# The last expert stage reads its stationary tiles as even and odd tokens instead of first and last 128

## What is computed

```python
ue = u_tab[eid]
a = jax.nn.gelu(jnp.einsum('thkd,td->thk', ue, xb).astype(jnp.float32))
ve = v_tab[eid]
return jnp.einsum('thk,thkd->td', (g * a).astype(xb.dtype), ve)
```

## Time and profile before

| | us |
|---|---|
| median of 3 runs | 2239.63 (2239.49 to 2239.93) |
| the profiled execution | 2239.02 |
| its span in the profile | 2237.3 |
| TensorE busy (PE) | 2216.5, 99% of the span |
| weight loads busy (PEld) | 2082.9, 93% |
| VectorE, ScalarE, GpSimd busy | 1704.3, 1353.4, 854.4 |

### The profile page before, as it was taken

One profiled execution on the slowest core, in us unless ns is written; L12 is line 12 of the kernel. 1 busy time (PEld: TensorE's weight loads), 2 busy tenths in 40 slices (PEclk: granted clock), 3 DMA queues, 4 the chain that ended last, 5 costly groups with the idle time before them and its releaser, 6 DMA issues.

```text
span 2237.3 us, 49289 instructions
## 1 busy us (share of the span) xinstructions
PE 2216.5 (99%) x15792; PEld 2082.9 (93%) x15792; DVE 1704.3 (76%) x3283; ACT 1353.4 (60%) x2705; POOL 854.4 (38%) x766
## 2 busy tenths in 40 slices
PE   8999999999999999999999999999999999999998
PEld 8999999999999888888999999999999998888887
DVE  6556768976888788788874567699578888888887
ACT  6544546667777555555764545566677775555555
POOL 3100108988777122121032001099877771221210
PEclk9999999999999999999999999999999999999999
DMA  6444554555444789888555445455554448898884
GB/s 225 162 143 164 168 181 160 188 186 181 159 159 160 259 306 324 271 304 298 176 187 164 141 166 188 137 189 187 183 178 159 159 161 284 311 321 267 306 279 138
DMA packets 127141, 462.94 MB, mean 207 GB/s; under 512 B 14704, under 2 KB 14864, under 8 KB 126288
## 3 DMA queue, kind: packets, MB, share of 16 engines
q1 hardware_dynamic: 106416, 385.20, 49.1%
q0 software_dynamic: 20640, 76.68, 12.1%
HBM read 457.87 MB, written 3.95 MB: 206 GB/s over the span
## 4 chain that ended last, share of the span: by engine, by line
PE 96%; DVE 2%; ACT 1%; issue 1%; POOLq 0%; POOL 0%; ACTq 0%; DVEq 0%
PE ps L1436 21%; PE ps L1441 20%; PE ps L1437 20%; PE ps L1674 10%; PE ps L1675 10%; PE ps L1676 10%; PE ps L1630 1%; PE ps L1631 1%; PE ps L1589 1%; PE ps L1552 0%; DVE w_lo L875 0%; POOLq L324 0%; DVE h_lo L914 0%; PE ps L1554 0%; PE ps L1535 0%
## 5 line engine op out<-in xcount | busy, mean ns | idle before, releaser
L398 POOL TENSOR_TENSOR w_lo<-raw,w_hi 128x512 fp32r<-128x512 f32 x508 | 644.9, 1292 | 251.9 <-ACT w_hi L499 156.3
L1436 PE MATMUL ps<-h_hi,w_hi 128*128 128x256 f32 (+1 forms) x2592 | 651.2, 289 | 10.1 <-DVE h_lo L856 7.9
L1437 PE MATMUL ps<-h_lo,w_hi 128*128 128x256 f32 (+1 forms) x2592 | 638.3, 282 | 0.0
L1436 PEld LDWEIGHTS ps<-h_hi,w_hi 128*128 128x128 f32 x2592 | 489.3, 189 | 11.5 <-issue 9.3
L1437 PEld LDWEIGHTS ps<-h_lo,w_hi 128*128 128x128 f32 x2592 | 487.8, 188 | 0.2
L477 ACT ACTIVATE w_hi<-raw 128x1024 fp32r<-128x1024 f32 x334 | 351.8, 1053 | 190.5 <-PE ps L1441 189.7
L1244 DVE TENSOR_TENSOR w_lo<-raw,w_hi 128x512 fp32r<-128x512 f32 x504 | 347.6, 690 | 120.4 <-ACT w_hi L725 83.0
L875 DVE TENSOR_TENSOR w_lo<-raw,w_hi 128x1024 fp32r<-128x1024 f32 x208 | 256.5, 1233 | 186.7 <-ACT w_hi L477 185.7
L1674 PE MATMUL ps<-w_hi,h_hi 128*128 128x512 f32 x1016 | 395.2, 389 | 0.0
L1676 PE MATMUL ps<-w_hi,h_lo 128*128 128x512 f32 x1016 | 395.2, 389 | 0.0
L1675 PE MATMUL ps<-w_lo,h_hi 128*128 128x512 f32 x1016 | 395.2, 389 | 0.0
(11 more groups left out here) (225 smaller groups left out, 2973.5 us busy)
## 6 DMA issues: line engine op xcount, KB each, us to landing
raw<-stream SPq DMA_DIRECT2D x730, 512.0 KB, 3.4
bias<-bias_in POOLq DMA_DIRECT2D x2, 1152.0 KB, 6.9
x_keep<-x POOLq DMA_DIRECT2D x2, 1152.0 KB, 5.3
x<-x_keep POOLq DMA_DIRECT2D x2, 1152.0 KB, 10.5
x<-x_in SPq DMA_DIRECT2D x4, 288.0 KB, 4.6
y_out<-t_op SPq DMA_DIRECT2D x4, 288.0 KB, 2.1
ws<-ws_in POOLq DMA_DIRECT2D x2, 512.0 KB, 4.2
ring<-u_rows,rows POOLq DMA_INDIRECT x44, 6.5
```

Of the source, the lines that this page charges most:

```text
L398: return pool.tensor_tensor(w_lo[:, k % 2, lo_col:hi_col], raw[:, k, lo_col:hi_col], w_hi[:, k % 2, lo_col:hi_col].bitcast(F32), ALU.subtract)
L1436: pe.matmul(out, wh, rhs_hi, start=first, stop=False)
L1437: pe.matmul(out, wh, rhs_lo, start=False, stop=False)
```

## The change

Tile 0 becomes the tokens 0, 2, 4, ..., 254 and tile 1 the tokens 1, 3, ..., 255. The stationary operand of every matmul of the stage is then 128 columns at a step of two (8 bytes apart), spread over the 1024 bytes of all 256 tokens. The moving operand, the PSUM banks, the number, shape and order of the instructions and all waits stay. `v_sum` holds even tokens in tile 0 and odd ones in tile 1; `turn` writes each transpose to every second column of its 256 PSUM columns, which puts the tokens back in order. What reads these columns is unchanged.

```diff
+                def every_second(tokens, tile):
+                    return tokens.rearrange("p (n i) -> p i n", i=TILES)[:, tile, :]
+
                 def expert_unit(q, j, e, first=False, last=False):
...
                         for tile in range(TILES):
-                            at = slice(tile * P, tile * P + P)
-                            m_up = m_first[:, 0, at] if first else mixed_hi[L][j][:, at]
-                            m_low = m_first[:, 1, at] if first else mixed_lo[L][j][:, at]
+                            m_up = every_second(m_first[:, 0, :] if first else mixed_hi[L][j], tile)
+                            m_low = every_second(m_first[:, 1, :] if first else mixed_lo[L][j], tile)
...
                 def turn(c):
                     out = ps[:, OUT_BANK[c], :]
                     for tile in range(TILES):
-                        pe.transpose(out[:, tile * P:tile * P + P], v_sum[:, tile, c * P:c * P + P], ident[:, :])
+                        pe.transpose(every_second(out[:, 0:SEQ], tile), v_sum[:, tile, c * P:c * P + P], ident[:, :])
```

## The result

| | median, us | runs |
|---|---|---|
| kernel before | 2239.78 (2239.49 to 2240.06) | 4 |
| changed kernel | 2260.12 (2259.99 to 2260.51) | 4 |

The ratio is 1.009, with a 95% interval of 1.0078 to 1.0102. The change costs 20.3 us. The time lies inside the range that was given, on the other side from the forecast.

A forecast was written before the change was run, and what follows sets the result against it. TensorE's distance between matmul starts was taken to bound the kernel. 2239.0 - 34 (loads) + 0 (transposes) = 2205.0 us, given as 2206 since the median of the runs stands 0.6 us higher; range 2199 to 2276.

The forecast's parts named there:

- What bounds the kernel: TensorE, busy 99% of the span; the last expert stage, 696.4 us, bound only by 226.7 ns between matmul starts.
- What the 226.7 ns are made of: Last expert stage: 213.3 ns for 512 columns plus 13.4 ns, of which about 11 ns disturbance between load and stream.
- the plain f32 rows: Plain f32 matmuls of 288 columns: 242.3 ns, only 2.3 ns over their columns; read as load and stream at one pace.
- The hint from the earlier trace: First unit of the stage, tiles from `m_first` 32 bytes off: 233 ns instead of 226.7, taken as a hint, no proof.
- The load: Stationary loads at step two, 3072 times: distance falls from 226.7 to 215.6 ns, 34 us gained.
- two readers at one pace: Load at step two walks 8 bytes in two cycles like the stream; they meet once, then no more: 11.1 ns less.
- the price doubles: Rival, slower (0.32): load and stream conflict per line or stretch, the wider walk has twice as many; 237.8 ns, 2274 us.
- half price: Half of the extra cost in the rival of conflicts per line or stretch: kernel time 2257 us.
- a load that takes twice as long: Last expert stage: at most 233.4 ns per matmul, 6.7 ns over the distance before, 21 us lost.
- Nothing changes: Rival, unchanged (0.20): the 11 ns are a fixed cost of changing a float32r tile, wherever it lies; 2239 to 2243 us.
- The transposes: 32 transposes writing every second PSUM column: taken as 0, at most 3.5 us lost.
- what is late next: VectorE, ScalarE and the DMA queue keep up with a stage of 331 us instead of 348, so the gain stays.

The follow-up runs named there:

- map_pair: Last expert stage with still tiles; upper and lower parts, second tile and moving operand moved separately: 213.4 to 220.0 ns per matmul at 480 columns, 226.7 to 233.3 at 512.
- the scan: Last expert stage with tiles from a still part of SBUF, starts moved within 256 bytes: step one 226.7 to 234.3 ns per matmul, step two 229.9 to 233.5.
- map_plain: Same tiles and streams read as plain f32, several steps and places: 429.2 ns at 512 columns; at 256 columns 215.8 ns, at step 4 233.3.
- before_moved_32: Kernel before, with only the four buffers of mixed_hi and mixed_lo moved by 32 bytes: 2260.18 us, ratio 1.0089.
- map_place: Last expert stage with still tiles at chosen steps and starts: step one 226.7 or 233.3 ns unmoved or moved 32 bytes, step two unmoved 233.3, step 8 244.4.

## Why the prediction was wrong, step by step

**What bounds the kernel** was right: the distance between two starts in that stage, and nothing else, carried the whole change, 3072 x 6.6 = 20.3 us.

**What the 226.7 ns are made of** was right in part. 213.3 ns belong to the columns, and what comes on top depends on how the two readers lie to each other (map_pair). But at steps one and two the runs move it only between 13.3 and some 22 ns. That 11 of the 13.3 ns of the kernel before are disturbance too was taken over from the plain f32 rows; at 512 columns no float32r variant fell below 226.7 ns, so this is not shown. The hint from the earlier trace rows was a good one: `m_first` lies 32 bytes off, and that place cost 233.3 ns in the scan too.

**The load is the step that failed.** The prediction held that two readers at one pace meet once and do not meet again, and took the plain f32 matmuls of the earlier trace rows for the proof. Those are undisturbed whatever the pace: with a stream that takes a column every second cycle, steps one, two and four all stand at 429.2 ns (map_plain). The equal pace was one of several differences between the rows that were compared, and the runs show that it was not the one that mattered. With a step of two the float32r distance was 229.9 to 233.5 ns at all 35 places tried, 14 to 18 ns over the 215.6 that were forecast. The load's pace itself, two cycles per column, was an upper bound (116.7 ns over 128 columns) taken for a value; no run measures it.

**The rival 'the price doubles'** had the sign and half of the size (6.6 of 11.1 ns; its half price, 2257, was 3 us off). Its mechanism, price per stretch, falls: the same price appears without any step after a move of 32 bytes. What the prediction did not list is what happened: the kernel before lay at one of the few cheap places, and the new arrangement left it. The row that could have said so was there: one unit at another place, 233 ns, and 6.3 ns dearer. It was used against another reading, and not asked what it would make of the sum by itself: 3072 x 6.3 = 19 us, close to the measured 20.3.

**Luck.** The prediction also priced a load that takes twice as long: at most 233.4 ns and 21 us lost. These are nearly the measured figures, but not for that reason: the load is recorded at 194 ns against 188, and before_moved_32 lost the same 20 us with loads at step one.

**'Nothing changes'** rested on the load costing nothing more, and on the 13.3 ns being fixed; they went to 20.0. The two rules of the Trainium skill behind it fare differently. The Trainium skill, SBUF — State Buffer, Specifications (TRN2), with two hits per 16-byte line for full bandwidth, agrees roughly with the loads themselves: 188 ns at four columns per line, 194 at two, and about 310 at one (step 4 in map_place). It says nothing of what a load does to the stream. The Trainium skill, TensorE: Matmul & The Clock Gate, Step-by-step: what each phase is for, speaks of two independent read ports; that the load leaves the stream alone does not follow for float32r here, where 480 columns took 213.4 to 220.0 ns by nothing but the place of the two operands.

**The transposes** (0, at most 3.5 us) and **what is late next** were right: 2.33 us for six turns, and nobody kept TensorE waiting.

**Left open**: which part of the loss is the start of the odd tile and which the step, why places within 256 bytes have the prices they have and so many of them the same three, why the cheapest place goes with the width of the stream, and why the changed kernel, moved by 64 bytes, did not get the price that the scan shows there.

## What to carry to other kernels

Where float32r matmuls follow each other with a new stationary tile each time, a matmul of 512 columns took 13 to 22 ns more than its columns here, at steps one and two, and where in this range it stood depended on where the two operands lie in SBUF against each other; a move of 32 bytes was worth 0.9% of this kernel. So before changing how a tile is read, scan its start over 256 bytes, judge a new access pattern against the average place and not against a place that happens to be good, and time the kernel itself at the place that the scan picks, since a scan of still tiles missed by 3 ns here. And when two rows differ in several things, an argument that uses one of them needs a row in which only that one differs.

## What was not expected of the hardware

Loads at steps of 3, 4 and 8 columns are recorded at 252, 310 and 329 ns, against 188 at step one, longer than the distance between two matmuls of 512 columns, which yet rose only to 235.5, 235.0 and 244.4 ns. Here are step 4 and step 8 in map_place (columns: busy us, mean ns of one; idle us).

```profile
L1682 PEld LDWEIGHTS ps<-w_hi,h_hi 128*128 128x128 f32 x41 | 12.7, 310 | 0.0
...
L1682 PEld LDWEIGHTS ps<-w_hi,h_hi 128*128 128x128 f32 x41 | 13.4, 327 | 0.0
```

Transposes that write every second f32 column of PSUM took the same 388 ns per turn as those that write adjoining ones.
